# adaLN products of a hybrid diffusion trunk: eight units ahead of block 0, the rest dealt over its units, gates computed in their own block

## The reference, cut to what matters

```
def _modulation(cond, w, b):
    m = jax.nn.silu(cond) @ w + b
    return m.reshape(cond.shape[0], 1, N_MOD, D_MODEL)      # N_MOD = 9
def _adanorm(x, g, shift, scale):
    return _rms(x, g) * (1.0 + scale) + shift
def _half_ffn(x, m, j0, g, wg, wu, wd):
    h = _adanorm(x, g, m[:, :, j0], m[:, :, j0 + 1])
    f = (jax.nn.silu(h @ wg) * (h @ wu)) @ wd
    return x + 0.5 * m[:, :, j0 + 2] * f
```

## Time and profile before

| what | us |
|---|---|
| median of three timed runs | 3329.4 |
| fastest of them | 3325.38 |
| the profiled execution | 3325.85 |
| its span, first to last instruction | 3323.7 |

### The profile page before, as it was taken

How to read it: one execution, slowest core, us unless ns; L and a number is a source line. 1 busy time by engine, 2 the same in 40 slices (tenths; PEclk the granted TensorE clock), 3 DMA queues, 4 the chain that set the end, 5 groups by cost and what they waited for, 6 DMA issues and landing times.

```text
span 3323.7 us, 52566 instructions
## 1 busy us (share of the span) xinstructions
PE 3164.4 (95%) x19204; PEld 2952.2 (89%) x19204; DVE 2468.0 (74%) x4229; ACT 1340.7 (40%) x2410; POOL 252.4 (8%) x381
## 2 busy tenths in 40 slices
PE   7999898899999999899999999999999999889997
PEld 7899897889999998868999998899999989888997
DVE  7888986668887885567887887688778887665444
ACT  2333566343333334354334333433433356634332
POOL 1000002600000000000000000000000000450000
PEclk9999999999999999999999999999999999999998
DMA  7555320134535553214453545345454531013332
GB/s 285 212 214 221 123 90 2 65 146 190 220 152 207 203 208 140 102 40 187 195 223 146 214 197 193 127 198 212 166 205 195 197 126 72 9 70 133 133 114 76
DMA packets 66011, 515.84 MB, mean 155 GB/s; under 512 B 8144, under 2 KB 16336, under 8 KB 18016
## 3 DMA queue, kind: packets, MB, share of 16 engines
q1 hardware_dynamic: 60512, 493.12, 38.2%
q0 software_dynamic: 5376, 21.04, 1.7%
HBM read 509.32 MB, written 4.82 MB: 155 GB/s over the span
## 4 chain that ended last, share of the span: by engine, by line
PE 87%; DVE 8%; ACT 2%; issue 2%; DMA 1%; POOL 0%; SPq 0%; DVEq 0%; ACTq 0%; POOLq 0%
PE bank L1798 77%; PE bank L1988 3%; PE bank L2000 2%; DVE xhat L1375 1%; DMA mod_raw<-mod_w 1%; DVE x L1379 1%; DVE split_lo L1225 1%; PE bank L1939 1%; DVE mod_junk L440 1%; PE bank L1994 1%; PE bank L1846 0%; DVE xS_lo L1318 0%; PE bank L1847 0%; DVE blocks L1494 0%; PE bank L1850 0%
## 5 line engine op out<-in xcount | busy, mean ns | idle before, releaser
L1798 PE MATMUL bank<-xS_hi,split_hi 128*128 128x386 f32 (+2 forms) x3280 | 1120.8, 342 | 13.4 <-DVE gate_n L1341 10.0
L1798 PE MATMUL bank<-xS_hi,split_lo 128*128 128x386 f32 (+2 forms) x3280 | 1111.7, 339 | 0.0
L1798 PE MATMUL bank<-xS_lo,split_hi 128*128 128x386 f32 (+2 forms) x3280 | 1110.4, 339 | 0.0
L1225 DVE TENSOR_TENSOR split_lo<-raw,split_hi 128x1024 fp32r<-128x1024 f32 x644 | 779.5, 1218 | 265.2 <-ACT split_hi L842 265.1
L842 ACT ACTIVATE split_hi<-raw 128x1024 fp32r<-128x1024 f32 x644 | 652.8, 1051 | 489.5 <-DMA raw<-ffn_w 346.9
L440 DVE SCALAR_TENSOR_TENSOR mod_junk<-mod_raw,cond 128x1024 f32<-128x1024 f32 x536 | 656.0, 1224 | 61.6 <-DVE mod_junk L440 33.9
L1798 PEld LDWEIGHTS bank<-xS_hi,split_hi 128*128 128x128 f32 (+1 forms) x3280 | 618.1, 188 | 28.6 <-DVE split_lo L1225 10.5
L1798 PEld LDWEIGHTS bank<-xS_lo,split_hi 128*128 128x128 f32 (+1 forms) x3280 | 618.8, 189 | 9.9 <-issue 0.4
L1798 PEld LDWEIGHTS bank<-xS_hi,split_lo 128*128 128x128 f32 (+1 forms) x3280 | 619.0, 189 | 1.0
L1798 PE MATMUL bank<-split_hi,hid_hi 128*128 128x512 f32 x1056 | 413.4, 392 | 1.6 <-DVE hid_lo L1353 1.6
L1798 PE MATMUL bank<-split_lo,hid_hi 128*128 128x512 f32 x1056 | 413.0, 391 | 0.0
(11 more groups left out here) (272 smaller groups left out, 3077.6 us busy)
## 6 DMA issues: line engine op xcount, KB each, us to landing
raw<-ffn_w SPq DMA_DIRECT2D x176, 1536.0 KB, 7.6
mod_raw<-mod_w SPq DMA_DIRECT2D x134, 1024.0 KB, 4.8
raw<-a_in_w SPq DMA_DIRECT2D x20, 1536.0 KB, 6.3
gate_bc<-gate_dram POOLq DMA_DIRECT2D x12, 1024.0 KB, 5.4
raw<-b_in_w SPq DMA_DIRECT2D x8, 1536.0 KB, 6.3
raw<-a_out_w SPq DMA_DIRECT2D x4, 1536.0 KB, 7.6
mod_first<-mod_w SPq DMA_DIRECT2D x5, 1024.0 KB, 21.8
mod_first<-mod_rows SPq DMA_DIRECT2D x5, 1024.0 KB, 23.7
```

What stands on the lines that cost most here:

```text
L1225: dve.tensor_tensor(split_lo[:, unit.slot, q, 0:w], raw[:, unit.slot, q, 0:w], f32(split_hi[:, unit.slot, q, 0:w]), ALU.subtract).then_inc ...
L1798: ins = pe.matmul(out, lhsT, rhs, start=start and i == 0, stop=stop and i == 2)
```

## The change

Eight units remain in the prologue (shift and scale of block 0): four on DVE, four on PE. On PE the condition becomes the stationary operand (two columns) and the map moves, 256 columns at a time: 8 matmuls for a unit give two rows, which ACT copies out and PE transposes back into columns. `cond` is no longer loaded on all partitions: one row is loaded, and PE spreads it with four matmuls (ones by row), from which ACT takes the SiLU. POOL sets its constants first and loads `tri`, `rope_tab` and `rows` later. Weight unit 0 is loaded in two transfers behind unit 7, then weight unit 1, then adaLN units 8 and 9.

Block 0 takes 24 units, dealt by the single product (`first_mods`): 3 products in the first step, then 4 or 5 in each step, 93 over 20 steps, none in the last. SP loads weight unit 2 ahead of them, and the load of each later adaLN unit stands at the place where its buffer comes free. Block 0 is written out on DVE and SP instead of looped. The vectors of all layers get a place of their own (`modv`), FFN 1 to 6 keep 18 units each, and FFN 7 takes the last 4 in its second and third pair of steps. The unit behind the norm of block 1 goes.

The gate of block r is computed inside block r: in an FFN in the last pair of steps, in kind a in the tail, in kind b at the start of attention, in kind c at the fourth channel tile. POOL stores and loads it there, ahead of the residual of the same block. `scales(r + 1)` stays where `gates(r + 1)` was.

```diff
-MOD_PROLOGUE = 3 * KT // MOD_TILES
-MOD_PER_FFN = 18
-MOD_ON_PE = (1, 3, 5, 7, 9)
+MOD_PROLOGUE = 2 * KT // MOD_TILES
+MOD_FFN0, MOD_PER_FFN, MOD_FFN7 = 24, 18, 4
+MOD_ON_PE = (1, 3, 5, 7)
 MOD_ON_DVE = tuple(m for m in range(MOD_PROLOGUE) if m not in MOD_ON_PE)
-MOD_FIRST, MOD_LAST = 3, 3
-assert MOD_PROLOGUE + MOD_FIRST + MOD_PER_FFN + MOD_LAST == MOD_UNITS
+MOD_AFTER_FFN0 = MOD_PROLOGUE + MOD_FFN0
+assert MOD_AFTER_FFN0 + 6 * MOD_PER_FFN + MOD_FFN7 == DEPTH * MOD_UNITS
...
+def first_mods():
+
+    columns = [(m, i) for m in range(MOD_PROLOGUE, MOD_AFTER_FFN0) for i in range(2 * MOD_TILES)]
+    upto = [0] + [3 + (len(columns) - 3) * j // (FT - 2) for j in range(FT - 1)] + [len(columns)]
+    return [columns[lo:hi] for lo, hi in zip(upto, upto[1:])]
...
-        sp.dma_start(cond[:].rearrange("p c k -> p (c k)"), inp["cond"].to_broadcast([P, 2 * D])).then_inc(cond_in, 16)
+        def load_first_ffn(ph):
+
+            load_unit(Unit(ph, 2))
+            for j, columns in enumerate(first_mods()):
+                if j + 3 < ph.units:
+                    load_unit(Unit(ph, j + 3))
+                elif j + 3 == ph.units and stages > 1:
+                    load_unit(Unit(by_stage[1][0], 0))
+                for m, i in columns:
+                    if i == 2 * MOD_TILES - 1 and m + 2 < MOD_AFTER_FFN0:
+                        load_mod(m + 2, m % 2)
+
+        sp.dma_start(cond_row[:], inp["cond"]).then_inc(cond_in, 16)
         sp.dma_start(cond_cols, inp["cond_cols"]).then_inc(cond_in, 16)
         for m in range(MOD_PROLOGUE):
             dst, landed, _ = mod_operand(m)
-            src = inp["mod_rows"][MOD_ON_PE.index(m)] if m in MOD_ON_PE else inp["mod_w"][0, m]
+            src = inp["mod_rows"][MOD_ON_PE.index(m)] if m in MOD_ON_PE else inp["mod_w"][m]
             sp.dma_start(dst.rearrange("p t c -> p (t c)"), src).then_inc(landed, 16)
-            if m >= MOD_PROLOGUE - 2:
-                load_unit(Unit(phases[0], m - MOD_PROLOGUE + 2))
+        first_w = inp["ffn_w"][0, 0]
+        sp.dma_start(raw[:, 0, 0], first_w[:, 0:PART]).then_inc(first_landed[0], 16)
+        sp.dma_start(raw[:, 0, 1:3].rearrange("p q c -> p (q c)"), first_w[:, PART:3 * PART]).then_inc(first_landed[1], 16)
+        load_unit(Unit(phases[0], 1))
+        load_mod(MOD_PROLOGUE, 0)
+        load_mod(MOD_PROLOGUE + 1, 1)
...
             if r == 0:
                 for t in range(NT):
                     norm_root(0, t)
-                gate_store(0)
-                gate_load(0)
+                pool.dma_start(tri[:], inp["tri"]).then_inc(tables_in, 16)
+                pool.dma_start(rope_tab[:], inp["rope_tab"]).then_inc(tables_in, 16)
+                pool.dma_start(rows[:], inp["rows"].to_broadcast([P, ROWS])).then_inc(tables_in, 16)
             if r == 6:
                 load_means()
             if kind == "a":
                 delta_net(r // 3)
+            gate_store(r)
+            gate_load(r)
             if kind == "b":
                 attention(r // 3)
                 mixer_root()
             if r == NORMS - 1:
                 pool.wait_ge(res_prod, 6 * (NORMS - 1))
                 pool.dma_start(final_row[:], inp["final_g"].to_broadcast([P, D])).then_inc(final_in, 16)
-            if r + 1 < NORMS:
-                gate_store(r + 1)
             residual_roots(r)
-            if r + 1 < NORMS:
-                gate_load(r + 1)
...
-        act.activation(cond[:], cond[:], ACT.Silu).then_inc(cond_ready, 1)
+        for i in range(4):
+            act.wait_ge(cond_spread, i + 1)
+            act.activation(cond[:, i // 2, 512 * (i % 2):512 * (i % 2) + 512], ps[i][:], ACT.Silu).then_inc(cond_ready, 1)
+
+        def copy_mod_row(i):
+
+            act.wait_ge(mod_mm, i + 1)
+            act.activation(mod_rows[:, i], ps[MOD_BANKS[i % 2]][0:2, 0:MOD_TILES * P], ACT.Copy).then_inc(mod_row_copied, 1)
+
+        copy_mod_row(0)
+        copy_mod_row(1)
...
-        act.wait_ge(*mod_count(6))
-        act.wait_ge(mod_mm, 3)
-        act.wait_ge(consts_in, 16 * CONSTS)
-        round_unit(Unit(phases[0], 0))
+        copy_mod_row(2)
+        round_part(Unit(phases[0], 0), 0)
+        copy_mod_row(3)
+        round_part(Unit(phases[0], 0), 1)
...
-        def vectors(r):
+        def biased(r, lo, hi):
 
             par, v0 = vec_of(r)
-            dve.wait_ge(*mod_count(mod_needed(r)))
-            v = modv[:, par, v0:v0 + 3 * KT]
+            dve.wait_ge(*mod_count(mod_needed(r, hi == 3 * KT)))
+            v = modv[:, par, v0 + lo:v0 + hi]
             b0 = COL_MOD_B + N_MOD * KT * (r // 3) + v0
-            b = cols[:, b0:b0 + 3 * KT].rearrange("p (k o) -> p k o", o=1).to_broadcast([P, 3 * KT, 2])
+            b = cols[:, b0 + lo:b0 + hi].rearrange("p (k o) -> p k o", o=1).to_broadcast([P, hi - lo, 2])
             steps.settle(dve.tensor_tensor(v, v, b, ALU.add))
 
         def gates(r):
 
-            if r:
-                vectors(r)
-                scales(r)
+            biased(r, 2 * KT, 3 * KT)
             par, v0 = vec_of(r)
             gate = modv[:, par, v0 + 2 * KT:v0 + 3 * KT]
...
+            biased(r, 0, 2 * KT)
...
+                if last:
+                    gates(r)
                 if last and r + 1 < NORMS:
-                    gates(r + 1)
+                    scales(r + 1)
...
-                    for step, m, slot, landed, layer in mod_steps(f, b, first, last):
+                    for step, m, slot, landed in mod_steps(f, b, first, last):
                         if step == u:
-                            mod_unit(dve, mod_raw[:, slot], mod_landed[slot], landed, m, layer, m - MOD_UNITS * layer)
-
-            bodies(dve, FT // 2, body)
+                            mod_unit(dve, mod_raw[:, slot], mod_landed[slot], landed, m)
+                    if f == 0:
+                        for m, i in first_mods()[j]:
+                            mod_one(dve, *mod_operand(m), m, i)
+
+            bodies(dve, FT // 2, body, unrolled=f in (0, 7))
...
+                    gates(3 * layer + 1)
                 if h == 3 and kind == "a" and 3 * layer + 2 < NORMS:
-                    gates(3 * layer + 2)
+                    scales(3 * layer + 2)
...
+            gates(3 * ph.index + 1)
...
+                if k == 3:
+                    gates(r)
...
+        dve.wait_ge(mod_turned, len(MOD_ON_PE))
+        for b, bank in enumerate(MOD_BANKS):
+            at = 2 * MOD_TILES * (1 + 2 * b)
+            of_pe = modv[:, 0].rearrange("p (u w) c -> p u (w c)", w=4 * MOD_TILES)[:, 0:2, at:at + 2 * MOD_TILES]
+            turned_of = ps[bank][:, MOD_TURNED_AT:MOD_TURNED_AT + 4 * MOD_TILES].rearrange("p (u w) -> p u w", u=2)
+            ins = dve.tensor_copy(of_pe, turned_of)
+        steps.settle(ins)
...
-                for step, m, slot, landed, layer in mod_steps(0, 0, False, True):
-                    if step == 2:
-                        mod_unit(dve, mod_raw[:, slot], mod_landed[slot], landed, m, layer, m - MOD_UNITS * layer)
...
-        pe.wait_ge(cond_ready, 1)
-        for i, m in enumerate(MOD_ON_PE):
-            weights, landed, count = mod_operand(m)
+        def mod_row(i):
+
+            weights, landed, count = mod_operand(MOD_ON_PE[i])
             w = weights.rearrange("p t c -> p (t c)")
             pe.wait_ge(landed, count)
+            if i >= 2:
+                pe.wait_ge(mod_row_copied, i - 1)
+            for k in range(KT):
+                ins = pe.matmul(ps[MOD_BANKS[i % 2]][0:2, 0:MOD_TILES * P], cond_cols[:, 2 * k:2 * k + 2], w[:, MOD_TILES * P * k:MOD_TILES * P * (k + 1)],
+                                start=k == 0, stop=k == KT - 1)
+            ins.then_inc(mod_mm, 1)
+
+        def turn_mod_row(i):
+
+            pe.wait_ge(mod_row_copied, i + 1)
             for t in range(MOD_TILES):
-                for k in range(KT):
-                    at = MOD_TILES * P * k + P * t
-                    ins = pe.matmul(ps[BANK_MOD][:, 4 * i + 2 * t:4 * i + 2 * t + 2], w[:, at:at + P], cond_cols[:, 2 * k:2 * k + 2],
-                                    start=k == 0, stop=k == KT - 1)
-            ins.then_inc(mod_mm, 1)
+                at = MOD_TURNED_AT + 2 * MOD_TILES * (i // 2) + 2 * t
+                ins = pe.transpose(ps[MOD_BANKS[i % 2]][:, at:at + 2], mod_rows[:, i, P * t:P * (t + 1)], ident[0:2, 0:2])
+            ins.then_inc(mod_turned, 1)
+
+        pe.wait_ge(pool_init, 1)
+        pe.wait_ge(cond_in, 32)
+        for i in range(4):
+            pe.matmul(ps[i][:], ones[0:1, :], cond_row[:, 512 * i:512 * (i + 1)], start=True, stop=True).then_inc(cond_spread, 1)
+        pe.wait_ge(cond_ready, 5)
+        mod_row(0)
+        mod_row(1)
         pe.wait_ge(consts_in, 16 * CONSTS)
-        pe.wait_ge(pool_init, 1)
+        turn_mod_row(0)
+        ffn_norm(0, 0)
+        mod_row(2)
+        turn_mod_row(1)
+        turn_mod_row(2)
+        mod_row(3)
+        turn_mod_row(3)
```

(56 more changed lines are left out.)

112 lines of the change are left out of this document (53 added, 59 removed).

## The result

The changed kernel takes 3294.16 us (median of 4 runs, 3292.21 to 3295.78); the kernel before, beside it, 3327.39 us. One of the four runs of the kernel before took 3548.86 us, in a slower state of the chip, and the ratio leaves it out. The ratio is 0.9904, 95% interval 0.9892 to 0.9915: 1% less time, which is less than the 2% that count as a difference here. The forecast was 3297 us, 3286 to 3313, and within 2% with a chance of 0.96. The profiled execution took 3295.78 us with a span of 3293.7, 30.0 us less than the span in the earlier trace rows; the sum of the prediction was 29.1.

A forecast was written before the change was run, and what follows sets the result against it. PE bounds the kernel (87% of the chain), so only its idle or low-clock stretches can give time. -16.8 + 0.3 - 12.3 - 0.3 = -29.1 from 3325.85 gives 3296.75, rounded to 3297 us; range 3286 to 3313.

The forecast's parts named there:

- Up to the first matmul of block 0: Prologue: 6.8 MB less ahead of the eighth unit, so scale_col comes earlier; 16.8 us saved.
- The unit price of 3.6 us: Prologue: time of one PE unit in the new form, taken between bounds of 2.2 and 6.9 us.
- the landing of the eighth unit: Prologue: with 10.8 MB ahead of it, PE's last unit lands at about 30.9 us.
- The half clock at the start of block 0: PE idles about 4 us ahead of block 0; 0.3 us more lost on top of the earlier 1.5.
- The hole at the third unit: Block 0: weight unit 2 issued earlier removes 10.04 us of idle PE and 2.3 of half clock; 12.3 us saved.
- The sentence on what is late next: Block 0: gate_n of unit 1, behind the first step's 3 products, fits by less than a microsecond.
- The deal: Block 0: 4.65 products a step take 12.53 us against PE's 12.58, so PE does not wait.
- the rival of the price of 1.39: Block 0: a product costs 1.39 us, a step 13.1 for 12.58; total 3306 us, chance 0.12.
- The end of block 0: The hid_lo stall grows from 1.59 to 4.1 us, the later wait falls from 7.09 to 4.29; net 0.3 gained.
- The gates: Gates in their own block: path of 9.9 us within 17.1, 7 spare, residuals do not wait; 0 us.
- the rival of the slower change: Residuals wait for gates whose path takes 25.6 us; 85 us lost, total 3382 us, chance 0.05.
- The rival of the half clock: Prologue: PE runs at 1.2 GHz, a unit costs 7.2 us, the 16.8 is lost; centre 3308 us, chance 0.12.

The follow-up runs named there:

- light end: Against the changed kernel, the last adaLN unit's four products go behind block 1's norm and step 20 has none; 3289.13 us, ratio 0.9886.
- control: The changed kernel run once more, unchanged; 3297.91 us, ratio 0.9913.

## Why the prediction was right, point by point

**The total was right; two terms were off in opposite directions, and that they nearly cancel is luck.** Taken apart at moments that both profiles have:

- *Up to the first matmul of block 0*: 56.33 to 37.73, a gain of 18.6, forecast 16.8 (a first matmul at 39 to 40). The unit price of 3.6 us was right to 0.02, as a choice between 2.2 and 6.9, of which the 6.9 was a price at half clock. What was off is the landing of the eighth unit: forecast at 30.9 from bytes and rate, but it landed at 28.7, and TensorE began on it at 29.37. The sum puts all of POOL's 2.39 MB ahead of it, although the change moves three tables, 0.43 MB, behind it; with them back in the prologue it landed at 31.5 and held TensorE, as forecast. So `scale_col` is set by TensorE's row of work from 18.56 on, which begins with a wait for a load; VectorE's products and low half are done 1.1 us before it (the wait at 33.76); and the loads, the forecast's bound, have 0.6 us to spare. That the products began at 10.74, for about 11, is luck: the spread of the condition began at 2.91 instead of 5.82, with no 1 MB load ahead of it, and took 7.16 us instead of 4.3, at half clock. Of the 18.6 us, runs price the tables (1.9 at the first matmul) and the old form (4.3, most of it clock); the four units, the condition and the first weights that no longer go ahead were not tried one by one.
- *The half clock at the start of block 0*: 0.3 on top, as forecast (10.78 us from the first matmul to the second unit, for 10.49).
- *The hole at the third unit*: gone, with its half clock: 25.42 us from the second unit to the fourth, for 38.11, a gain of 12.7 where 12.3 were forecast. The reason given was a part of it. That the load was issued behind adaLN loads holds, but with that alone mended 5.48 us of waiting stay, for the eight products of the first step. The sentence on what is late next, and why the first step has few products, named the other half without pricing it.
- *The deal*: no wait of TensorE from 61 to 303 us, as forecast; the products stand 1.265 us apart in straight-line code, so the rival of the price of 1.39 is out. The light end, with 4.68 a step instead of 4.65, already had a wait of 1.3 us.
- *The end of block 0*: forecast 0.3 gained, in truth some 3 lost (31.1 us ahead at the eleventh unit, 28.1 at the first projection). The stall was 5.12 instead of 4.1. TensorE's waits from there to the first projection come to 10.2 us, where they were 10.0 before; the rest of the loss, 2.9, is the clock, which the forecast left out: behind the stall TensorE ran at 0.82 (303 to 322) and 0.50 (329 to 335) of its clock. In the kernel before, the same place was at full clock, stall and all (338 to 350, above). From the end of the stall to the first projection it is 18.36 us, 0.5 less than before (344.60 to 363.45), though the wait for `xhat` is 2.7 shorter. This is the term that failed, by its size; the run with the light end gives back 5.7.
- *The gates*: nothing, as forecast. Their margin is real, and so is the price of missing it, 59 us in eight blocks, where the rival of the slower change had 85 in eleven paths. In block 6 the margin is 2.8 us and not the forecast's 7.
- *Behind block 0*: forecast nothing; 1.9 us more were gained. The control shows that two executions of one kernel differ by more there, so this is not a gain of the change.

**The rival of the half clock** was set aside for a wrong reason. The prediction read the clock of 1.00 from 14 to 48.3 us as evidence that TensorE was at full speed in the prologue; the lengths of like instructions, and a record of the clock that begins with a rise at 54.12, show that it was at half. For the same reason a clock of 1.00 on the page could not have told right from wrong ahead of 14.61 us in the changed kernel. The Trainium skill, page TensorE: Matmul & The Clock Gate, part 1, which has half rate as the default, is borne out here (5.33 us for the first PE unit and 3.62 for the next), and the prediction's sentence that the trace does not bear it out falls. The rival's time was nevertheless wrong: only the spread of the condition and a part of the first unit ran slowly, and the transposes cost 2.84, not 10.7 (5.36 was their price at half clock already), since TensorE was at full clock from 14.61 on.

## What to carry to other kernels

A wait names the instruction that came last, not every cause: at the third unit a late load and a long queue of products stood one behind the other, and either alone left well over half of the hole. When one cause of a wait is removed, work out when the next thing in line would be ready and give it its own price. Work dealt evenly into an engine with no room to spare should end a step or two before the block does, where the next engine waits for its last result; and price a stall with the slower clock that follows it.

## What the runs showed of the hardware that was not expected

- A page's clock of 1.00 ahead of the first recorded change is no measurement: the record begins with a rise at 54.12, 28.45 and 14.61 us in three kernels, and under a 1.00 throughout the 24 transposes of x took 5.36, 4.12 and 2.84 us, by what TensorE had done before. The length of a known instruction is the better clock.
- The old form, a stream of weight loads with matmuls of two columns, ran at 6.9 us a unit for as long as it lasted (34.4 us for five in the kernel before), and at 4.29 once the transposes had gone before it.
- Three loads of 128 to 160 KB each, 0.43 MB, among 1 MB loads made the last of these land 2.6 us later; their bytes at 420 GB/s are 1.0 us.
- In the DeltaNet's stretch of short dependent steps the mean clock differs from run to run (0.74 to 0.91 in 20 us), and the whole mixer by up to 3.7 us; three edits of 1 to 2 us could be told only at the first projection.
